# A gated linear attention's blocks: inner products first, then the states; the scores in two banks by row half

## The reference, cut to what matters

```python
att = jnp.einsum('bhnid,bhnjd->bhnij', qc * jnp.exp(b - b_mid), kc * jnp.exp(b_mid - b))
att = jnp.where(causal, att, 0.0)
o_intra = jnp.einsum('bhnij,bhnjv->bhniv', att, vc)
...
o_inter = jnp.einsum('bhnid,nbhdv->bhniv', qc * jnp.exp(b), states)
o = (o_intra + o_inter)
```

## Time and profile before

| | |
|---|---|
| median of 3 runs | 702.7 us (701.09 to 705.27) |
| the profiled execution | 701.69 us, of which span 699.9 us |
| TensorE (PE) busy | 668.8 us, 96% of the span |
| VectorE (DVE) busy | 384.5 us, 55% |
| ScalarE (ACT) busy | 201.9 us, 29% |
| GpSimd (POOL) busy | 106.1 us, 15% |
| mean granted clock of TensorE | 0.988 of 2.4 GHz |

### The profile page before, as it was taken

One profiled execution on the slowest core, in us unless ns is written; L12 is line 12 of the kernel. 1 busy time (PEld: TensorE's weight loads), 2 busy tenths in 40 slices (PEclk: granted clock), 3 DMA queues, 4 the chain that ended last, 5 costly groups with the idle time before them and its releaser, 6 DMA issues.

```text
span 699.9 us, 11236 instructions
## 1 busy us (share of the span) xinstructions
PE 668.8 (96%) x4523; PEld 513.1 (73%) x4523; DVE 384.5 (55%) x717; ACT 201.9 (29%) x426; POOL 106.1 (15%) x139
## 2 busy tenths in 40 slices
PE   4999999999999999999999993999999999999997
PEld 2579999888788888888779992656656575756564
DVE  4547224687888777776764546352615253452514
ACT  5336122213534434342343333111111202020111
POOL 3400006787500000000000011110101010110010
PEclk9999999999999999999999996899999999999999
DMA  7432112301112121111347105999999999999953
GB/s 238 134 120 62 62 61 65 117 1 61 61 61 61 60 61 61 61 61 60 103 139 301 61 31 201 411 415 401 415 402 413 406 410 408 403 420 401 418 217 120
DMA packets 50086, 139.33 MB, mean 199 GB/s; under 512 B 6354, under 2 KB 28387, under 8 KB 41844
## 3 DMA queue, kind: packets, MB, share of 16 engines
q1 hardware_dynamic: 47298, 134.36, 50.4%
q0 software_dynamic: 2592, 4.20, 1.6%
q10 hardware_dynamic: 146, 0.07, 0.0%
HBM read 139.66 MB, written 4.19 MB: 206 GB/s over the span
## 4 chain that ended last, share of the span: by engine, by line
PE 86%; DVE 6%; ACT 3%; issue 2%; DMA 2%; POOL 0%; ACTq 0%; DVEq 0%; POOLq 0%
PE bank L880 16%; PE bank L562 13%; PE bank L563 12%; PE bank L564 12%; PE bank L893 8%; PE bank L998 8%; PE bank L789 2%; DVE y_lo L1702 1%; PE bank L762 1%; PE bank L788 1%; PE bank L787 1%; PE bank L722 1%; PE bank L726 1%; ACT whi L1101 1%; DVE sig_a L1440 1%
## 5 line engine op out<-in xcount | busy, mean ns | idle before, releaser
L1378 DVE TENSOR_TENSOR wlo<-wraw,whi 128x2048 fp32r<-128x2048 f32 (+1 forms) x26 | 58.6, 2256 | 30.4 <-ACT whi L1101 30.4
L562 PE MATMUL bank<-whi,xhi 128*128 128x256 f32 (+1 forms) x256 | 73.3, 286 | 0.0
L563 PE MATMUL bank<-wlo,xhi 128*128 128x256 f32 (+1 forms) x256 | 71.8, 280 | 0.0
L564 PE MATMUL bank<-whi,xlo 128*128 128x256 f32 (+1 forms) x256 | 71.8, 280 | 0.0
L562 PE MATMUL bank<-xhi,whi 128*128 128x512 f32 (+2 forms) x176 | 69.0, 396 | 1.6 <-DVE wlo L1378 1.6
L563 PE MATMUL bank<-xlo,whi 128*128 128x512 f32 (+2 forms) x176 | 67.6, 387 | 0.0
L564 PE MATMUL bank<-xhi,wlo 128*128 128x512 f32 (+2 forms) x176 | 67.2, 386 | 0.0
L880 PE MATMUL bank<-wgate,xgT 128*64 128x256 f32 x512 | 60.4, 390 | 1.3 <-DVE xgT L1660 1.0
L880 PE MATMUL bank<-wup,xgT 128*64 128x256 f32 x512 | 58.4, 381 | 0.0
L893 PE MATMUL bank<-wdown,hT 128*64 128x512 f32 x256 | 58.1, 595 | 0.0
L1101 ACT ACTIVATE whi<-wraw 128x2048 fp32r<-128x2048 f32 (+1 forms) x26 | 47.8, 1842 | 25.5 <-PE bank L564 18.7
(11 more groups left out here) (291 smaller groups left out, 1308.8 us busy)
## 6 DMA issues: line engine op xcount, KB each, us to landing
wgate<-in_expert_w_gate SPq DMA_DIRECT2D x32, 1024.0 KB, 9.1
wup<-in_expert_w_up SPq DMA_DIRECT2D x32, 1024.0 KB, 11.2
wdown<-in_expert_w_down SPq DMA_DIRECT2D x32, 1024.0 KB, 17.8
wraw<-in_w_in SPq DMA_DIRECT2D x17, 1024.0 KB, 5.5
wraw<-in_w_out SPq DMA_DIRECT2D x4, 1024.0 KB, 5.2
h<-in_x SPq DMA_DIRECT2D x4, 512.0 KB, 5.0
wraw<-in_w_gla_branch SPq DMA_DIRECT2D x2, 1024.0 KB, 5.2
wraw<-in_w_attn_branch SPq DMA_DIRECT2D x2, 1024.0 KB, 5.0
```

Of the source, the lines that this page charges most:

```text
L562: nc.tensor.matmul(ps, lhi(k), rhi(k), start=(k == 0), stop=False)
L563: nc.tensor.matmul(ps, lhi(k), rlo(k), start=False, stop=False)
L564: last = nc.tensor.matmul(ps, llo(k), rhi(k), start=False, stop=(k == kt - 1))
L1378: nc.vector.tensor_tensor(w_view(wlo[split_buffer(c)], c), w_view(wraw[c % 2], c), w_view(whi[split_buffer(c)], c).bitcast(F32), ALU.subtr ...
```

## The change

In `attT` each row half (two heads) takes a bank of ring S of its own, and the link between the halves is gone. VectorE's product with the mask becomes two, one for each half. In `glao` the four inner products come first, then the eight products with the states in the head order (0, 2, 1, 3), with the link after head 2 kept. Only the very first inner product has `start`, and the `stop` flag stands at head 3's products with the states. The number of matmuls stays.

```diff
                 elif kind == "attT":
                     b = step[1]
-                    ps = banks.take(pe, "S", step)
+                    for half in range(2):
+                        name = ("attT", b, half)
+                        ps, a = banks.take(pe, "S", name), half * GK
+                        for j in range(2):
+                            last = nc.tensor.matmul(ps[:, j * P:(j + 1) * P], g_k1[a:a + GK, j, b * P:(b + 1) * P],
+                                                    g_q1[a:a + GK, j, b * P:(b + 1) * P], start=True, stop=True)
+                        last.then_inc(banks.done(name), 1)
+                elif kind == "glao":
+                    b = step[1]
+                    ps = banks.take(pe, "O", step)
+                    for half in range(2):
+                        pe.wait_ge(*banks.emptied(("attT", b, half)))
+                    pe.wait_ge(*banks.emptied(("kv", 2 * b)))
+                    for hd in range(GH):
+                        nc.tensor.matmul(ps[:, hd * GV:(hd + 1) * GV], att[b % 2][:, hd, :], vg[:, b, hd * GV:(hd + 1) * GV],
+                                         start=(hd == 0), stop=False)
                     for hd in (0, 2, 1, 3):
                         a = (hd % 2) * GK
-                        last = nc.tensor.matmul(ps[:, hd * P:(hd + 1) * P],
-                                                g_k1[a:a + GK, hd // 2, b * P:(b + 1) * P],
-                                                g_q1[a:a + GK, hd // 2, b * P:(b + 1) * P], start=True, stop=True)
-                        if hd == 2:
-                            link(last)
-                    last.then_inc(banks.done(step), 1)
-                elif kind == "glao":
-                    b = step[1]
-                    ps = banks.take(pe, "O", step)
-                    pe.wait_ge(*banks.emptied(("attT", b)))
-                    pe.wait_ge(*banks.emptied(("kv", 2 * b)))
-                    for hd in (0, 2, 1, 3):
-                        a = (hd % 2) * GK
-                        o = ps[:, hd * GV:(hd + 1) * GV]
-                        nc.tensor.matmul(o, att[b % 2][:, hd, :], vg[:, b, hd * GV:(hd + 1) * GV],
-                                         start=True, stop=False)
                         for s in range(2):
                             t0 = b * P + s * GC
                             last = nc.tensor.matmul(ps[s * GC:(s + 1) * GC, hd * GV:(hd + 1) * GV],
                                                     g_q3[a:a + GK, hd // 2, t0:t0 + GC],
                                                     st[a:a + GK, 2 * b + s, hd // 2, :],
-                                                    start=False, stop=True)
+                                                    start=False, stop=(hd == 3))
                         if hd == 2:
                             link(last)
                     last.then_inc(banks.done(step), 1)
...
                 elif kind == "attT":
                     b = step[1]
-                    dve.wait_ge(*banks.filled(step))
                     if b >= 2:
                         dve.wait_ge(*banks.filled(("glao", b - 2)))
-                    nc.vector.tensor_tensor(att[b % 2][:, :, :], banks.get(step)[:, :].rearrange("p (h i) -> p h i", h=GH),
-                                            C("att_mask").unsqueeze(1).to_broadcast([P, GH, P]), ALU.mult)\
-                        .then_inc(banks.read(step), 1)
+                    for half in range(2):
+                        name = ("attT", b, half)
+                        dve.wait_ge(*banks.filled(name))
+                        nc.vector.tensor_tensor(att[b % 2][:, half:GH:2, :], banks.get(name)[:, 0:2 * P].rearrange("p (h i) -> p h i", h=2),
+                                                C("att_mask").unsqueeze(1).to_broadcast([P, 2, P]), ALU.mult)\
+                            .then_inc(banks.read(name), 1)
```

## The result

The changed kernel takes 695.73 us (median of 7 runs, 694.49 to 698.73) against 702.43 us for the one before (7 runs, 700.38 to 705.27). The ratio is 0.9916, with a 95% interval of 0.9893 to 0.9940: 0.8% faster, beyond what can be mistaken for no change.

A forecast was written before the change was run, and what follows sets the result against it. TensorE was taken to bound the kernel at the change and right behind it. 3.0 us from attT plus 3.6 from glao less 0.1 of wait make 6.5, so 702.7 becomes 696.2 us; range 693.4 to 699.2, forecast's chance 0.74.

The forecast's parts named there:

- The halves of attT run side by side: attT on TensorE: without the link, 0.65 us a block instead of 1.41, as in step S; 3.0 us saved.
- rival (a): attT: the halves follow each other, 0.97 to 1.19 us a block, 0.9 to 1.8 saved; kernel 697.9 us; chance 0.13.
- The change of shape costs: glao on TensorE: fewer crossings between matmul shapes make 2.26 us a block instead of 3.17; 3.6 us saved.
- Rival (d): glao: reordering does nothing, crossings cost the same anywhere, glao keeps 3.17 us; kernel 699.8 us; chance 0.05.
- The flags `start` and `stop`: glao: start on the first head alone and stop on the last change no instruction's size; costed at nothing.
- The wait at attT(1): TensorE at attT(1) waits about 0.1 us for VectorE's second product to empty its bank; 0.1 subtracted.
- The cover: Between VectorE's product with the mask and glao(0): 5.1 us, of which 3.5 are left with the change.
- VectorE's two products: The mask's product split in two adds about 0.1 to 0.2 us a block, 0.6 in all, on VectorE.
- Nobody else is late: GpSimd's q for qT(3) keeps 9 us of cover; merged steps on TensorE have no wait to 320 us.
- The clock further on: Half-clock stretch from 424 to 440.6 us may shift against the first expert matmuls: plus or minus 1.5 us.
- (b): Experts' stage: its loads set the pace and begin no sooner, so the gain is given back; 702.7 us; chance 0.05.
- (c): The half-clock stretch grows: 13 us more uses up the gain, 20 more makes 706.2 us; chance 0.03.

The follow-up runs named there:

- The run with the wait: Changed kernel, but TensorE waits between the halves of the scores until the first half's bank is full; 698.11 us against 701.41 for the kernel before.
- glao alone: Changed kernel with only glao's new order, scores in one bank with the link as before; 698.29 us against 701.41 for the kernel before.
- two crossings: Changed kernel with glao by row half, two changes into the states' shape instead of one; 696.37 us against 701.41 for the kernel before.
- late scores: Changed kernel with a 128x512 VectorE reciprocal ahead of block 0's products with the mask; 701.43 us against 702.65 for the kernel before.
- second comparison: Changed kernel unaltered, run again on another chip beside the kernel before; 695.76 us against 702.65.
- the scores alone: Changed kernel with only the new scores step, glao's order as before; 698.69 us against 701.41 for the kernel before.
- its variant with late scores: Kernel before with a 128x512 VectorE reciprocal ahead of block 0's product with the mask; 701.75 us against 702.65 without it.
- glao in two banks: Changed kernel with glao's output in two banks, no link, ScalarE copying in two pieces; 692.12 us against 702.65 for the kernel before.
- the half delay: Changed kernel with a 128x256 VectorE reciprocal ahead of block 0's products with the mask; 697.89 us against 702.42 for the kernel before.

## Why the prediction was right

1. **The halves of attT run side by side.** Forecast 0.65 us a block, measured 0.65, and step S was the right row to read it from. Saved 3.0 less the wait, 2.9 alone and 2.9 by taking it back. Rival (a), that the halves follow one another, is out; so is, for this kernel, the strict reading of the Trainium skill's sentence on program order (TensorE: Matmul & The Clock Gate, "Step-by-step: what each phase is for"): the fifth matmul in program order started 0.01 us behind the first. The run with the wait has 1.41 us for order with a wait between the halves; order without a wait would have been the 0.97 to 1.19 of rival (a).
2. **The change of shape costs, and the new order takes three of four away.** Forecast 2.26 us, measured 2.29; 3.5 us saved in place of 3.6. The rows were glao's own steps and kv. Rival (d) is out by the run with glao alone. The flags `start` and `stop` were costed at nothing; no run changes them alone, but two crossings, with the new flags, came within 0.01 us of a sum from rows with the old ones.
3. **The wait at attT(1).** Forecast 0.1 us, measured 0.11. It was treated as a small sum to subtract. The late scores show that it is more than that: in the kernel before a product late by 3.4 us costs nothing, in the changed one 4.9. The cover that the prediction looked at, the 3.5 us ahead of glao(0), is not the nearest one any more. VectorE's two products take 0.75 us for one of 0.68, 0.07 more a block, where the prediction added 0.1 to 0.2.
4. **Nobody else is late.** Beyond the 0.11 us at attT(1) no wait for VectorE, none for GpSimd, and from 170 to 313 us TensorE without a gap.
5. **The sum.** 6.5 us forecast, 6.4 in the stretch, 6.7 between the medians. The 0.03 us a block on glao make the 0.1. The median of the kernel before is 702.43 us over seven runs where the forecast had started from 702.7 over three; that and the 0.2 us between 6.5 and 6.7 make the distance of 695.73 from 696.2.
6. **The clock further on** was given as plus or minus 1.5 us. In the profiled execution it went against the change, 0.9 us over the experts and up to 1.0 ahead of them, where the wait for the gathered rows is longer too; which part of the latter is the clock's is not shown. The medians, 6.7 us apart and 6.9 in the second comparison, show nothing given back of the 6.4. Whether the longer half-clock stretch goes with the change stays open. It had 20.5 us in both traces of the changed kernel, in the scores alone and in the late scores of the changed kernel. It had 17.1 in the kernel before and its variant with late scores, but also in glao alone, two banks with the wait, two crossings, glao in two banks and the half delay. So neither part of the change brings it every time. Two readings of rows 1 and 15 were off: the page shows two slices under full clock, 6 and 8 tenths, not one, and the low stretch ended at 441.47 us, over the first 4.1 us of expert matmuls, not at 440.6. Rivals (b) and (c) are out: the experts' stage kept its length but for that half of the clock's overlap and started sooner, and the low stretch grew by 3.4 us where (c) needed 13.

## What to carry to other kernels

A wait on one's own matmul costs more than the drain where it stands between two halves of the array: taking it away by giving each row half its own bank let the halves run at once, worth 0.76 us of 1.41 for eight small matmuls, and again 0.7 us in glao; look in the trace for another step of the same form to price it. Matmuls of one tile shape belong together, and where a link must stay, a change of shape right behind it was the cheapest here. When a step takes a second bank of a ring, it inherits the wait for that bank's last reader: check its slack at the next user of the ring, not only at the reader of the result, since a short wait can cost twice its length: here one of 1.5 us on TensorE cost 3.3, and 1.5 of that through the clock.

## What the runs showed of the hardware that I had not expected

An idle time of TensorE of 1.5 us, in an otherwise dense stream, was followed by 1.2 GHz for about 3.4 us, as an idle time of 3.1 us was; before both it had been busy without a gap. The clock fell 0.2 us behind the end of the longer wait and 1.5 us behind the end of the shorter one, and cost some 1.4 and 1.5 us. An idle time of 1.18 us elsewhere was not followed by it. Four tiles of 64 by 64, two on each bank, did not slow each other: 16 instructions in 0.61 us against 8 on two tiles in 0.58. And in the scores as in step S, the first matmul of one row half starts 0.01 us behind the first of the other, although three instructions of that other half stand between them in the program.
